# Dilated attention: the upper query operand copied on chip by GpSimd instead of loaded

## The reference, cut to what matters

```
s = jnp.einsum('bgnqhd,bgnkhd->bgnhqk', qs, ks).astype(jnp.float32) + bias
s = jnp.where(mask[:, None], s, NEG_INF)
lse = jax.nn.logsumexp(s, axis=-1)
p = jnp.exp(s - lse[..., None]).astype(v.dtype)
o = jnp.einsum('bgnhqk,bgnkhd->bgnqhd', p, vs)
```

## Time and profile before

| what | value |
|---|---|
| median of 3 runs | 5713.83 us (5705.85 to 5720.06) |
| the profiled execution's own time | 5713.3 us |
| its span, first to last instruction | 5711.7 us |
| granted TensorE clock over the span | 0.953 of full speed |
| busy share of the span: PE, DVE, ACT, POOL | 91%, 68%, 51%, 18% |
| first score matmul and last q and k score of dilated attention | 1551.0 us and 2147.8 us |
| q and k and v loads of the phase | queue q1 on SyncE |

### The profile page before, as it was taken

The page is one execution under the profiler, slowest core; times in us unless marked ns, Lnnn a source line. Parts: engine busy times, 40 slices in busy tenths (PEclk is TensorE's granted clock), DMA queues, the critical chain, the costliest instruction groups (busy, mean ns, idle before and its releaser), DMA issues. The chain is left out here.

```text
span 5711.7 us, 110333 instructions
## 1 busy us (share of the span) xinstructions
PE 5183.3 (91%) x36030; PEld 4421.8 (77%) x36031; DVE 3864.3 (68%) x6739; ACT 2924.9 (51%) x4917; POOL 1056.6 (18%) x936
## 2 busy tenths in 40 slices
PE   6999999999899997969999947998999897999993
PEld 5888798998888885858888836988888685888883
DVE  5678887778655557776877756775444555765886
ACT  3343444344377775554656533343777312654764
POOL 2010020000000000043544411110000002543552
PEclk9999999999999998979999978999999897999997
DMA  5877776456599997578998856665455335987996
GB/s 169 217 195 211 195 204 170 125 149 151 158 320 312 318 305 223 175 274 280 316 326 261 277 173 192 178 185 152 136 153 153 131 133 196 321 259 228 360 322 227
DMA packets 874798, 1261.29 MB, mean 221 GB/s; under 512 B 184638, under 2 KB 545517, under 8 KB 874412
## 3 DMA queue, kind: packets, MB, share of 16 engines
q1 hardware_dynamic: 747420, 908.75, 51.9%
q0 software_dynamic: 72272, 276.84, 15.9%
q10 hardware_dynamic: 54720, 70.60, 3.8%
HBM read 941.20 MB, written 333.67 MB: 223 GB/s over the span
## 5 line engine op out<-in xcount | busy, mean ns | idle before, releaser
L522 PE MATMUL qa_ps_out<-qa_x_hi,qa_w_hi 128*128 128x512 f32 x1344 | 532.9, 397 | 37.9 <-DVE qa_w_lo L646 20.6
L522 PE MATMUL qa_ps_out<-qa_x_lo,qa_w_hi 128*128 128x512 f32 x1344 | 528.3, 393 | 0.0
L522 PE MATMUL qa_ps_out<-qa_x_hi,qa_w_lo 128*128 128x512 f32 x1344 | 527.8, 393 | 0.0
L559 ACT ACTIVATE qa_w_hi<-qa_w_whole 128x1024 fp32r<-128x1024 f32 x180 | 191.2, 1062 | 452.6 <-DVE qa_w_whole L637 252.3
L522 PE MATMUL qa_ps_out<-qa_w_hi,qa_x_hi 128*128 128x256 f32 x1344 | 383.0, 285 | 8.9 <-DVE qa_w_lo L646 8.9
L522 PE MATMUL qa_ps_out<-qa_w_lo,qa_x_hi 128*128 128x256 f32 x1344 | 381.7, 284 | 0.0
L522 PE MATMUL qa_ps_out<-qa_w_hi,qa_x_lo 128*128 128x256 f32 x1344 | 381.6, 284 | 0.0
L2599 DVE CUSTOM_DVE_ANT_0 ga_minus_s<-ga_ps_s,ga_bias 128x512 f32<-128x512 f32 (+1 forms) x256 | 194.1, 758 | 257.6 <-PE ga_ps_s L2538 190.7
L1087 ACT ACTIVATE da_prob<-da_minus_s,da_rows 128x256 f32<-128x256 f32 (+1 forms) x768 | 317.6, 464 | 45.7 <-DVE da_rows L1055 45.5
L1055 DVE CUSTOM_DVE_ANT_0 da_minus_s<-da_ps_s,da_bias 128x256 f32<-128x256 f32 (+1 forms) x768 | 259.9, 376 | 110.9 <-PE da_ps_s L986 95.9
L522 PEld LDWEIGHTS qa_ps_out<-qa_x_hi,qa_w_hi 128*128 128x128 f32 x1344 | 255.2, 190 | 98.3 <-DVE qa_w_lo L646 27.1
(11 more groups left out here) (489 smaller groups left out, 15338.0 us busy)
## 6 DMA issues: line engine op xcount, KB each, us to landing
a_ex_w_raw<-w SPq DMA_DIRECT2D x128, 1024.0 KB, 8.0
b_ex_w_raw<-w SPq DMA_DIRECT2D x128, 1024.0 KB, 9.1
qa_w_raw<-w_qkv_a SPq DMA_DIRECT2D x144, 512.0 KB, 4.2
a_ex_w_raw<-w POOLq DMA_DIRECT2D x66, 1024.0 KB, 9.8
b_ex_w_raw<-w POOLq DMA_DIRECT2D x66, 1024.0 KB, 8.1
da_q_cross<-qT SPq DMA_DIRECT2D x48, 1024.0 KB, 9.7
da_k_parts<-kT SPq DMA_DIRECT2D x48, 1024.0 KB, 9.1
a_mn_o_in<-o SPq DMA_DIRECT2D x16, 1584.0 KB, 8.5
```

What stands on the lines that cost most here:

```text
L522: done = pe.matmul(out, stationary, moving, start=(k == 0 and i == 0), stop=(k == KH - 1 and i == 2))
L559: act.activation(w_hi[:, p % W_RING], src, ACT.Copy).then_inc(w_hi_done, 1)
```

## The change

`qk_loads` leaves out the two `q_top` DMAs per set, so a set is two DMAs and N_QK is 2 instead of 4. GpSimd makes `q_top` instead: after a set has landed it copies the 64 upper rows of each head from `q_cross` to the other 64 partitions of `q_top`, 1024 elements long, as two instructions per set. PE waits for these copies as well before the first score of a set. The zeroed halves, the matmuls and their order are as before.

```diff
         padded = sem("padded")
         q_zeroed = sem("q_zeroed")
+        top_made = sem("top_made")
...
-                out = [(q_cross[:, g], q), (k_parts[:, g, :, REACH:REACH + SEQ], k)]
-                for head in range(2):
-                    keep = slice(HD * high_place(1, head), HD * high_place(1, head) + HD)
-                    out.append((q_top[keep, g, head, :],
-                                scratch.qT[s * N_DIL + g, 2 * hp + head, high_place(0, head)]))
-                return out
+                return [(q_cross[:, g], q), (k_parts[:, g, :, REACH:REACH + SEQ], k)]
+
+            def top_rows(g, head):
+
+                to, of = (slice(HD * high_place(kind, head), HD * high_place(kind, head) + HD) for kind in (1, 0))
+                return q_top[to, g, head, :].bitcast(F32R), q_cross[of, g, head, :]
...
+                for u in range(len(units)):
+                    for g in range(N_DIL):
+                        pool.wait_ge(qk_loaded[g], 16 * N_QK * (u + 1))
+                        for head in range(2):
+                            to, of = top_rows(g, head)
+                            made = 2 * (N_DIL * u + g) + head
+                            if made:
+
+                                pool.wait_ge(top_made, made)
+                            else:
+                                pool.wait_ge(padded, 6)
+                            pool.tensor_copy(to, of).then_inc(top_made, 1)
...
                     if n % SEQ_TILES == 0:
                         pe.wait_ge(qk_loaded[g], 16 * N_QK * (u + 1))
+                        pe.wait_ge(top_made, 2 * (N_DIL * u + g + 1))
```

## The result

The changed kernel takes 5643.74 us, median of 4 runs (5642.79 to 5644.69), against 5711.82 us (5705.85 to 5720.06, 4 runs) of the kernel before on the same chip: a ratio of 0.9879, 95% interval 0.9865 to 0.9893. The direction was right, and with it little else: of the terms of the sum, the relief by fewer bytes and the lead of a set were wrong and the slow clock was priced too low, as the experiments show.

What follows compares the result with a forecast made beforehand. It took PE's waits for late upper-query loads in a full DMA queue as the bound; stalls 19.2, odd units 2.2, unit 0 3.0 and clock 6 sum to 30.4 us off 5713.3, forecasting 5683 us, range 5663 to 5707.

Steps and rivals of the forecast that it cites:

- Step (1): DMA queue: 96 loads, 25.2 MB, go; at 311 GB/s 1.7 us per set, 5 us per unit.
- r: Relief for a late set from fewer bytes queued ahead: one earlier set's share, 1.7 us; ends 0 and 5.
- step (2): Set loads: a set is complete at `k_parts`, on average 4.0 us before PE started with the upper queries there.
- step (4): PE's stalls at set starts: each shrinks 3.0 us, 19.2 us gained; four slow-clock stretches go, 1.5 us each, 6 us.
- Step (3): GpSimd: two copies follow each set, 2.7 us with hand-overs, costing nothing on the path except at a late set.
- c: Time of one GpSimd copy of 64 x 1024, taken as 1.2 us.
- C: Time of a set's two GpSimd copies with hand-overs, taken as 2.7 us; ends 2.2 and 5.1.
- Step (5): Phase's first set: first scores wait for `k_parts` and two copies; within a microsecond or two, costed at nothing.
- all stalls go: Rival: the DMA queue stops being full and every PE stall goes, 48.3 us off, 5665 us; chance 26%.
- The copies did not cost the gain: Rival judged here: GpSimd copies eat the lead, each stall changing by only -0.6 us, 5707 us; chance 16%.
- the dear copy: Rival: GpSimd copies crossing partition halves take 4.8 us each, some 55 us more, 5768 us; chance 5%.
- the lock: Rival: GpSimd and VectorE shut each other out; 5733 us if the copies also eat the lead; chance 3%.

Runs made afterwards that it cites:

- more_bytes: Kernel before, its own upper-query loads kept, plus 96 unread half-width spare loads (25.2 MB) behind their sets: 5843.8 us.
- bytes_behind: Changed kernel with the 96 removed loads (25.2 MB) put back behind each set, into a tile nobody reads: 5718.2 us, ratio to before 1.0003.
- bytes_ahead: Changed kernel with the 96 unread spare loads issued ahead of `q_cross` and `k_parts` of their set: 5741.5 us.
- no_copies: Changed kernel without GpSimd's 96 copies, upper operand left zero, so values change: 5679.1 us whole, 461.1 us in the fourteen-unit stretch against 459.4.
- copies_x4: Changed kernel with each GpSimd copy made four times in a row, a set's copies taking 8.7 us: 5685.7 us.
- full_width: Changed kernel with the removed 25.2 MB back, unread, as one 512 KB DMA over 128 partitions per set: 5652.7 us, again 5655.3.
- middle_rows: Changed kernel with 96 unread 64-row loads (25.2 MB) behind the sets, all landing in partitions 32 to 95: 5652.7 us.
- short_rows: Changed kernel with the 96 unread loads back behind the sets, rows 64 elements long instead of 1024 (1.6 MB): 5642.6 us.

## Why the prediction was wrong

**What bounds the kernel** was read rightly as far as it went: waits at the starts of even units, a queue that is full throughout. The changed kernel has none of them.

**Step (1), bytes, failed; this is the main error.** I priced 25.2 MB at the mean 311 GB/s, 5 us per unit, and took r = 1.7 us for a late set. The mean was the wrong price, because it depends on where a load lands: the 166 MB with full-width or middle-row loads pass at 357 and 358 GB/s, while the half-width ones of more_bytes cost as much as 185 GB/s would. At 358 GB/s the 165 MB of the kernel before would have taken 461 us, next to PE's 459 (an estimate; no run has exactly these bytes in that form): by it the kernel before was short not of bandwidth for its bytes but only for their form. A hint stood in my own step (2): the 0.52 MB of `q_top` landed 4.0 us after `k_parts`, where step (1) gave the same bytes 1.7 us. Other transfers can lie between the two, so it is a hint and no proof. The v loads ahead of a set were issued in 6.8 us less (11.6 to 4.9 on average), where r had 1.7.

**Step (2), the lead, failed.** I took 4.0 us per late set for the earlier completion, by subtracting the landing of `k_parts` in the kernel before, and paid the copies from it in step (4). But `k_parts` did not keep its landing time: 13.4 us after its issue at the even units instead of 11.8, in bytes_behind and in the changed kernel. With the copies a set is ready 0.4 us sooner after its issue than before, not 4.0 - 2.7 = 1.3 us sooner, and bytes_behind has no gain. The order itself is not worthless, as bytes_ahead shows with 23 us.

**Step (3), the copies, right but for size**: c = 1.03 us, not 1.2, C = 2.1, and hidden everywhere but at the first set, as no_copies shows. The two neighbours were the right ones, the memset at 0.97 the better. **Step (5), the start**, was right too: the first score came at 1551.7 us instead of 1551.0.

**Step (4), the slow clock, under-sized.** I took 1.5 us per long stall, 6 us in all; PE's busy time fell by 17.8 us in the stretch. copies_x4 measures a tail apart: 2.5 us each. Seven times 2.5 us is 17.5, close to the 17.8: in the kernel before seven waits of over 1.5 us have a clock of 0.50 to 0.67 in the 5 us behind them: the five that I counted and two more, of 2.17 us (0.66) and 1.96 us (0.66, no releaser). I had taken the first score's 0.39 us for a sign that the clock holds after 2.17 us, and it was none. The length of a wait alone does not tell either: behind one of 2.10 us the clock was 1.00.

**The floor was wrong.** I took unit 9, 33.93 us, for a unit without loss; a unit takes 32.8. It had a PE busy time of 33.18 in my own row, so 0.75 us of it was visibly idle. Over 16 units the difference is 18 us, which no case of mine could give: the rival "all stalls go" was the right case, at 26%, and its price of 48 us, too, was short of the 64.5.

**The rivals.** The copies did not cost the gain, though in bytes_behind they took all but 0.4 us of what lead there was; the dear copy did not come (1034 ns, crossing from one half of the partitions to the other costs little if anything: the memset took 974); the lock did not come (bias pass 375 ns, 376 without copies). The range was too narrow above all because its better end was a sum of the stalls that the trace names. The tail of the clock and the small gaps have no such name, and in the changed kernel both are gone with the stalls.

## What to carry to other kernels

Before pricing bytes in a full DMA queue, look at which partitions each transfer writes: the same bytes, as 64 rows in partitions 0 to 63 and 64 to 127, cost 56 us here beyond their cost in partitions 32 to 95 or over all 128, and that is the load to copy on chip, to merge or to move first. This kernel has more of them: the two v loads of g = 0 in each unit, 256 KB each, go to partitions 64 to 127 and 0 to 63 (`v_loads`), 8.4 MB in all, and the changed kernel still has them; no run tried to change that. For the best case of a change that removes stalls, take PE's busy time at full clock for a fixed number of instructions, not the span of a stretch that seems free of loss; and compare only the phase where an experiment changes values and later work depends on them.

## What I had not expected

- **Small gaps of PE go with the full queue, not with the stalls.** Before the transposes and outputs PE has waits with no releaser ("issue"), 10.8 us in the stretch before, 14.1 and 18.3 in the two traces of bytes_behind, none in the changed kernel. copies_x4 has stalls of 21.3 us and a DMA share of 0.90, and none of these gaps either. How large they are varies: 4.7 us in bytes_ahead, 1.6 to 4.4 in full_width and middle_rows. The queue q8 (instruction) moves 0.93 MB in 57 packets in the stretch, before and after alike; that PE's instructions come late through the same busy engines would fit, and is not shown.
- **A full queue scatters more than a bound PE.** Runs of the kernel before spread over 22.6 us (5705.9 to 5728.4 in 14), those of bytes_behind over 26 us, those of the changed kernel and of full_width over 2 us each and of middle_rows over 4 us. short_rows, also bound by PE in the stretch, has 9.6 us between its two runs; where they differ was not followed.
- **The DMA share does not tell whether the queue delivers.** It is 1.05 to 1.06 in more_bytes, in the kernel before and in full_width, at 293, 319 and 358 GB/s.
